# The order of the steps around one weight stream in a two-block transformer kernel

## The reference

```python
# first block, RWKV time mix (per layer), 8 heads of 64
w = -jax.nn.softplus(-(w0 + jnp.tanh(xw) @ w_up)) - 0.5
a = jax.nn.sigmoid(a0 + xa @ a_up)
kk = kk / jnp.maximum(jnp.sqrt(jnp.sum(kk * kk, axis=-1, keepdims=True)), 1e-12)
decay = jnp.exp(-jnp.exp(hs(w)))
state = (state * w_t[:, :, None, :] + sa[..., None] * b_t[:, :, None, :] + v_t[..., None] * k_t[:, :, None, :])
# first block, merge of the branches
branch = jnp.einsum('bsnw,nwd->bsnd', ys, w_branch[l])
merged = jnp.sum(gates * branch, axis=2)
x = x + gt1[:, None, :] * (merged @ w_out[l])
# second block, mixer
y_attn = window_attention(q, k, v, sink[i], rel_bias) @ w_attn_out[i]
c = depthwise_conv(c_val * jax.nn.sigmoid(c_gate), conv_w[i], conv_b[i])
y_conv = jax.nn.silu(layer_norm_2(c, conv_ln_g[i], conv_ln_b[i])) @ w_conv_out[i]
h = h + (g_attn * y_attn + g_conv * y_conv) @ w_o[i]
```

## Time and profile before

| | us |
|---|---|
| median of 3 runs | 2118.98 (2118.73 to 2119.17) |
| the profiled execution, time | 2120.44 |
| its span | 2118.5 |
| PE busy | 2095.2 (99%) |
| DVE busy | 1639.5 (77%) |
| ACT busy | 1235.6 (58%) |
| PE idle (span less busy) | 23.3 |

### The profile page before, as it was taken

One profiled execution on the slowest core, in us unless ns is written; L12 is line 12 of the kernel. 1 busy time (PEld: TensorE's weight loads), 2 busy tenths in 40 slices (PEclk: granted clock), 3 DMA queues, 4 the chain that ended last, 5 costly groups with the idle time before them and its releaser, 6 DMA issues.

```text
span 2118.5 us, 39184 instructions
## 1 busy us (share of the span) xinstructions
PE 2095.2 (99%) x16348; PEld 1902.0 (90%) x16348; DVE 1639.5 (77%) x2519; ACT 1235.6 (58%) x2010; POOL 13.1 (1%) x20
## 2 busy tenths in 40 slices
PE   8999999999999999999999999999999999999999
PEld 7898999999998899998888989888898888998888
DVE  7899789888887788877887656787688765778876
ACT  4754755555755656555655448566475644766554
POOL 0000000000000000000000000000000000000000
PEclk9999999999999999999999999999999999999999
DMA  9566567768644467655555654555555567455553
GB/s 371 198 210 216 175 214 256 243 226 288 224 158 171 163 209 239 204 181 188 188 190 189 230 159 154 203 190 189 189 180 189 189 196 223 140 170 209 189 189 130
DMA packets 122099, 424.57 MB, mean 200 GB/s; under 512 B 13457, under 2 KB 22033, under 8 KB 121154
## 3 DMA queue, kind: packets, MB, share of 16 engines
q1 hardware_dynamic: 121922, 422.06, 59.0%
HBM read 417.68 MB, written 4.33 MB: 199 GB/s over the span
## 4 chain that ended last, share of the span: by engine, by line
PE 90%; ACT 4%; DVE 4%; DMA 1%; issue 1%; POOL 0%; SPq 0%; ACTq 0%; DVEq 0%
PE bank L207 89%; ACT arena L258 2%; DVE arena L213 2%; DMA raw<-W 1%; ACT hi L258 1%; DVE lo L213 1%; PE bank L210 1%; ACT L258 1%; DVE arena L221 0%; DVE ada L230 0%; ACT L250 0%; DVE m L213 0%; DMA xT<-x 0%; ACT ych L258 0%; POOL arena L213 0%
## 5 line engine op out<-in xcount | busy, mean ns | idle before, releaser
L207 PE MATMUL bank<-h,hi 128*128 128x256 f32 (+1 forms) x5248 | 1183.2, 312 | 0.0
L258 ACT ACTIVATE hi<-raw 128x1024 fp32r<-128x1024 f32 x656 | 688.3, 1056 | 537.5 <-PE bank L207 468.4
L207 PE MATMUL bank<-h,lo 128*128 128x256 f32 x3328 | 950.2, 286 | 1.2 <-DVE arena L221 0.7
L207 PEld LDWEIGHTS bank<-h,hi 128*128 128x128 f32 x5248 | 861.4, 190 | 61.1 <-issue 2.6
L213 DVE TENSOR_TENSOR lo<-raw,hi 128x1024 fp32r<-128x1024 f32 x656 | 792.4, 1220 | 99.4 <-ACT hi L258 98.5
L207 PEld LDWEIGHTS bank<-h,lo 128*128 128x128 f32 x3328 | 633.7, 190 | 12.3 <-issue 7.3
L207 PE MATMUL bank<-act,hi 128*128 128x512 f32 x1056 | 370.0, 393 | 0.0
L207 PE MATMUL bank<-act,lo 128*128 128x256 f32 x1056 | 294.7, 279 | 0.0
L207 PEld LDWEIGHTS bank<-act,hi 128*128 128x128 f32 x1056 | 197.9, 187 | 47.3
L207 PEld LDWEIGHTS bank<-act,lo 128*128 128x128 f32 x1056 | 197.9, 187 | 0.0
L258 ACT ACTIVATE arena<-arena 128x256 f32<-128x256 f32 (+4 forms) x202 | 98.6, 493 | 159.6 <-DVE arena L213 151.5
(11 more groups left out here) (152 smaller groups left out, 1942.0 us busy)
## 6 DMA issues: line engine op xcount, KB each, us to landing
raw<-W SPq DMA_DIRECT2D x664, 512.0 KB, 4.0
ada<-WA SPq DMA_DIRECT2D x80, 512.0 KB, 3.7
arena<-WA SPq DMA_DIRECT2D x16, 512.0 KB, 14.2
arena<-conv_rows SPq DMA_DIRECT2D x16, 280.0 KB, 6.4
arena<-taps SPq DMA_DIRECT2D x2, 1792.0 KB, 8.8
p_projected<-arena SPq DMA_DIRECT2D x2, 1024.0 KB, 7.9
arena<-scr SPq DMA_DIRECT2D x16, 128.0 KB, 5.1
arena<-p_projected SPq DMA_DIRECT2D x2, 1024.0 KB, 4.9
```

Source lines behind the costliest of these rows:

```text
L207: return self.done(lambda e: e.matmul(out, l, r, start=start, stop=stop, skip_group_check=True))
L258: return self.done(lambda e: e.activation(out, in_, f, scale=scale, **kw))
```

## The change

Five changes of order; no instruction computes anything else than before.

1. In layer 0 of the time mix everything from "length" on comes one tick later (an added "next"); the transposes of B and K come one further tick later in both layers, behind "bonus". The number of ticks up to ("until", ("ln", l)) stays.
2. In each chunk "inv0" comes ahead of "x" in the same tick (four places).
3. In the convolution's chain "split" comes one tick later.
4. "branch0",3 and "branch1",0 change places.
5. On ACT the merges of a conv-out item are those of its own pair (0, 1 in item 0), where they were those of the pair before, the last two at the end of item 3.

```diff
 def rwkv_steps(l):
-    s = [("mix",), ("square",), "next", "next", ("lora", 0), ("lora", 1), "next", ("length",), "next", ("decay",), ("gate",),
-         "next", ("scan", 0), "next", ("scan", 1), "next", ("middle",), "next", ("powers",), "next", ("until", ("z", l, 5)), ("keys",), "next",
-         ("rate",), ("tok", "V", 0), "next", ("scale",), ("tok", "V", 1), "next", ("receive",), ("tok", "B", 0), "next",
-         ("bonus",), ("tok", "K", 0), "next", "next", "next", ("until", ("ln", l)), ("bonus sum",), "next", ("flag", ("prep", l))]
+    s = [("mix",), ("square",), "next", "next", ("lora", 0), ("lora", 1), "next"] + ["next"] * (1 - l)
+    s += [("length",), "next", ("decay",), ("gate",), "next", ("scan", 0), "next", ("scan", 1), "next", ("middle",), "next",
+          ("powers",), "next", ("until", ("z", l, 5)), ("keys",), "next", ("rate",), ("tok", "V", 0), "next", ("scale",), ("tok", "V", 1), "next",
+          ("receive",), "next", ("bonus",), ("tok", "B", 0), "next", ("tok", "K", 0), "next"] + ["next"] * l
+    s += [("until", ("ln", l)), ("bonus sum",), "next", ("flag", ("prep", l))]
     for c in range(2):
-        s += [("cross", c, 0), "next", ("cross", c, 1), "next", ("unit", c), ("until", ("gmlp", l)), ("level0", c), "next", ("x", c),
-              ("inv0", c), "next"]
+        s += [("cross", c, 0), "next", ("cross", c, 1), "next", ("unit", c), ("until", ("gmlp", l)), ("level0", c), "next", ("inv0", c),
+              ("x", c), "next"]
...
 def conv2_steps(l):
-    return s + ["next"] * (18 - s.count("next")) + [("mean",), "next", ("square",), "next", "next", ("var",), "next", ("norm",), ("silu",), "next", ("split",)]
+    return s + ["next"] * (18 - s.count("next")) + [("mean",), "next", ("square",), "next", "next", ("var",), "next", ("norm",), ("silu",), "next", "next", ("split",)]
...
-        s += [("branch1", l, 0), ("pause if", (l, 4)), ("branch0", l, 3), ("merge", l, 0), ("branch0", l, 4), ("branch1", l, 1), ("branch0", l, 5),
+        s += [("branch0", l, 3), ("pause if", (l, 4)), ("branch1", l, 0), ("merge", l, 0), ("branch0", l, 4), ("branch1", l, 1), ("branch0", l, 5),
...
                 elif what == "conv out":
                     l, p = q
                     f.tiles(8)
-                    for m in (2 * p - 2, 2 * p - 1) if p else ():
-                        a.wait_ge(v_main, ("conv out", l, m // 2))
-                        merge("m2", l, m, mh)
-                    for m in (6, 7) if p == 3 else ():
-                        a.wait_ge(v_main, ("conv out", l, 3))
+                    a.wait_ge(v_main, item)
+                    for m in (2 * p, 2 * p + 1):
                         merge("m2", l, m, mh)
```

## The result

The changed kernel's median is 2126.29 us in 13 executions, against 2119.08 for the kernel before: ratio 1.0027, 95% interval 1.0020 to 1.0034. The forecast was 2120.2 (2117.0 to 2122.6). The single executions don't lie around one value: one at 2120.88, four at 2122.0 to 2122.3, eight at 2125.6 to 2127.1. With each comes the mean clock granted to PE: 1.000, 0.999, and 0.998 to 0.996.

What follows compares the result with a forecast made beforehand. The tensor engine was taken as the bound, running 2095.2 of 2118.5 us. Gains of 4.13 and losses of 5.32 made it 1.2 us slower, 2120.2 us against the 2118.98 median, range 2117.0 to 2122.6.

Steps and rivals of the forecast that it cites:

- the price is x itself: At the four inverses PE waits for VectorE's masks, then runs x: 1.08 us per chunk 0, 2.12 per chunk 1.
- the sum: All terms together: gains 4.13 us, losses 5.32, net 1.2 us slower.
- the merges: Convolution output: merges in their own item end PE's 0.85 us wait in wo, gaining 0.95 us in each layer.
- A: At the inverses PE passes the waiting inv0 or masks come in time; exchange costs nothing, 2113.8 us; chance 0.09.
- B: In layer 0's front VectorE catches up altogether and PE keeps the 3.24 us: 2117.3 us; chance 0.09.
- C: In the convolution stage merges make ScalarE's copies late, so 2.3 us are not won: 2122.5 us; chance 0.11.
- D: In layer 0 decay stands behind a high copy whose weight block lands late: 4.9 us lost, 2125.1; chance 0.08.
- the front: Layer 0's later length sums and token transposes: VectorE's masks for the first inverse come 1.46 us earlier, lower bound 0.
- a restart of the pipeline: Small extra beside a removed PE wait: 0.87 us counted as 0.95 at y1, 0.85 as 0.95 in wo.
- 0.2%: Whole kernel: 4.2 us, taken as the least a measurement can tell from no change; chance of landing within 0.82.
- The late split: Convolution: PE's 0.91 us wait goes, a shorter one comes before conv out,0; 0.2 us gained per layer.

Runs made afterwards that it cites:

- x_first_c1: The changed kernel with x ahead of the identity step again only in chunk 1 of each layer: 2117.24 us, ratio 0.9992.
- filled_c1: The changed kernel with 48 needless small identity multiplications in front of chunk 1's waiting identity step: median 2121.68 us, ratio 1.0017.
- the two single-place kernels: The changed kernel with x ahead of inv0 everywhere except chunk 1 of one layer: 2118.04 us (layer 0) and 2119.49 us (layer 1).

## Why the prediction was wrong

- **The step that failed: "So the price is x itself: 1.08 for a chunk 0, 2.12 for a chunk 1."** PE stood about as long as that said (2.13 and 2.17 us against 2.12, 1.59 and 1.05 against 1.08), but a stand of chunk 1 has a second price: behind it the granted clock fell to half for 0, 3.4 or 6.8 us, 0, 1.7 or 3.4 us of time. The prediction had no term for the clock and no rival with it: its page showed full speed in all slices, and in that profile PE never stood longer than 1.67 us after its start. The sizes of the other terms don't explain it: with every gain at nothing the sum gives 2118.98 + 6.40 = 2125.4, still under the 2126.29, and most of the gains were there. x_first_c1, filled_c1 and the two single-place kernels show it from four sides. Taking the loss off the profiled executions gives 2122.28 - 1.7 = 2120.6 and 2127.01 - 6.8 = 2120.2, near or at the forecast. The Trainium skill, "TensorE: Matmul & The Clock Gate", section "What's actually happening", says that this clock has two levels, set by how busy PE has lately been; the 0.50 and 1.00 agree.
- **The rest of the sum held, in part by luck.** The two executions in which the changed kernel kept its clock took 2120.88 and 2120.87 us, 0.7 from the 2120.2. In the profiles, PE's lead against before went from 0.37 us behind chunk 0 of layer 0 (forecast 0.38) to a lag of 1.83 in front of chunk 1's levels (1.74) and 1.22 behind them (1.24). The first of these agrees so well because both are read against the same late execution: in the profile with the merges alone PE came to that place at 127.83, 1.51 earlier than the 129.34 of the trace of before. By their medians, merges that gave more than their term and a front that gave less made up for each other.
- **Rivals.** A: out, PE does stand. B: out by the 1.59 us before the masks, though of the earlier trace rows only 0.20 is left. C: out, PE waits for no high or low block at conv out. D: out, the high copy that had been at 70.31 came at 65.23, and decay started at 66.83. All four priced waits; none changed PE's speed.
- **Sizes.** By the medians the merges gave 2.7 us for 1.9, and the front 0.9 for 1.46; both differences are within the intervals of some 2 us either way. For the front the traces give a reason, argued and not shown by a run of its own: an extra of that one execution of before stood in the very rows that I took for typical. The forecast's range also left out the lower bounds of 0 that it gave for the front and for the merges; with both its upper end would have been 2125.4 too. The 0.1 us for a restart of the pipeline had no row beside it; the first record behind a wait takes 0.36 to 0.39 us where a like one within a row of work takes 0.28, which bears it out. And 0.2% isn't the least that can be told from no change: the interval of the result is 0.07% either way.
- **The late split** turned the wait of attention out,2 into one before conv out,0 (0.91 into 0.71), as forecast.

What stays open: why the same stand is followed by none, a short or a long loss in different executions. In the seven losses profiled the length goes with the moment of the fall: the five long ones began from 0.1 us before the stand's end to 0.6 after it, the two short ones 1.6 after it; what sets that moment no run shows. Nor does any run put a stand of 2.1 us at another place than a chunk 1, so that its length alone decides is not shown either.

## What to carry to other kernels

A step that needs nothing belongs ahead of the step that waits: in the in-order queue of the engine that sets the end it costs nothing there, and its whole length behind it. Price a stand of PE twice, by its length and by the clock afterwards, and look at the clock of single executions when their times fall into groups. A wait read from one profiled execution is worth checking against how far that execution lies above the median.

## What the runs showed of the hardware

- Stands of PE of 2.13 to 2.18 us, from a granted clock of 1.00 and between stretches of steady work, were enough for it to fall to 0.50: behind seven of the ten in the kept profiles, in layer 1 behind all five, in layer 0 behind two of five. Behind the twelve stands of 1.05 to 1.60 us in the same profiles and in those of x_first_c1 and filled_c1 it stayed 1.00, and in x_first_c1 the mean was 1.0 in 11 of 11.
- The slow stretches behind these stands were 3.4 us (two) or 6.8 us (five) long, and lay behind the stand, not in it: they began at its end or up to 1.6 us later, and ran on with PE busy again.
- Behind PE's last record of an execution, where it has no more work, the clock fell after 1.9 to 5.1 us in the fourteen profiles.
